# Gate/up tile pairs of a fused MLA decoder layer: six of sixteen k tiles as three 2x2 blocks, with one of four weight sums made by an adding DMA

## The chip, the core and the metric

The kernel runs on one core of a Trainium2 chip. The time is device microseconds of one launch. Engines work beside one another and meet only at semaphores: TensorE (PE) multiplies, ScalarE (ACT) and VectorE (DVE) work on elements, GpSimd (POOL) works on elements and issues software DMAs, SyncE (SP) issues hardware DMAs. A matmul's other half, the load of its 128x128 stationary operand, is PEld.

## What is computed

One layer: sparse latent attention, LayerNorm, SwiGLU, LayerNorm, on 256 tokens of width 2048, all in float32.

```python
def _swiglu(x, w_gate, w_up, w_down):
    return (jax.nn.silu(x @ w_gate) * (x @ w_up)) @ w_down
...
x = _layer_norm(DEEPNORM_ALPHA * x + m, ln1_g, ln1_b)
x = _layer_norm(DEEPNORM_ALPHA * x + _swiglu(x, w_gate, w_up, w_down), ln2_g, ln2_b)
```

The case is about `x @ w_gate` and `x @ w_up`: 256x2048 by 2048x5632, twice.

## The kernel before

**Splitting.** PE multiplies in a reduced float32 form (`float32r`). To keep float32 accuracy each operand is split into a high part and a rest, and each product is three matmuls: high by high, high by low, low by high. For weights, ACT copies the raw float32 block into `w_hi` (the conversion keeps the high part) and DVE then makes `w_lo = raw - w_hi`. So each block of weights goes SP's DMA, ACT, DVE, PE. One split of 128x1024 is a *step*. Steps are numbered by v. `hi_done` and `lo_done` count them. The split weights stand in a ring of four places (`RING`); ACT may fill a place only when PE has finished the step that held it four steps earlier (`used_step(v - RING)`).

**Tiles.** FFN columns go in 22 tiles of 256 gate and 256 up columns (a PSUM bank of 512 for each half of the tokens). Tile 0 and tile 1 are plain: 16 k tiles (128 rows of weights each), as 8 halves of two k tiles. Tiles 2 to 21 go in ten pairs p = 1 to 10 (`first` and `second` tile).

**Pairs.** In a pair, four k tiles (`PAIR_K`) are done as two 2x2 blocks in Winograd's form of Strassen's scheme. Rows of the 2x2 are token halves, columns are the two tiles, the inner index is the two k tiles of a block: seven products (P1, P5, P6, P7, P2, P3, P4) where eight would be needed. Each product is one step and six matmuls, three for each of the two blocks. The other twelve k tiles are plain, two to a step: `first` 0 to 5 and `second` 0 to 5, of 12 matmuls each. That is 7 x 6 + 12 x 12 = 186 matmuls of 128x512 and 19 steps to a pair. The products need four sums of weight blocks, made in place by DVE in `pair_sum` (line 1381), each 128x1024: T1 = B11 + B12, T3 = B12 + B22, T2 = T1 + B22, T4 = B21 + T2 (the minus signs of the scheme lie in the activations' sums and the seeds). P5 takes T1, P6 T2, P7 T3, P4 T4. They also need sums of activations, made once by POOL (lines 1568 to 1580, `g_sum`, `s_gate`).

**Seeds.** P1, P1+P6 and P1+P6+P7 begin other outputs: ACT copies a PSUM bank into another (line 984, semaphore `seeded`), and PE waits for that before it adds there. P5 goes to a bank of its own; ACT takes it out as `y_s` (line 990) and DVE adds it in twice (`add_y`, lines 1398 and 1400).

**Hidden units.** After a tile ends ACT makes the silu (line 935) and DVE multiplies by up (`gate_up`, line 1340). When both tiles of a pair are done DVE transposes them in the next pair in four groups of four 32x256 transposes (`turn_hid`, line 1353; one group after each of the steps `first` 2, 3, 4, 5). The last group raises `ffn_turned`. POOL waits for it and makes four sums for the down projection's own 2x2 blocks (lines 1587 to 1593), later one low part (line 1595), for seven of the pairs; ACT copies the high part (`hid_hi`, line 941), DVE makes the low part (`hid_lo`, line 1359).

**Order.** `ffn_sequence` writes out the order of steps; all engines follow it. The last three steps of a pair's second tile stand between the first products of the next pair. So P1, second 3, P5, second 4, P6, second 5, P7, P2, P3, first 0, P4, first 1 to 5, second 0 to 2, and again. SP's queue is one: plain halves into four places of 512 KB, the blocks of the next pair (two DMAs of 1 MB, `load_quad`) after the plain loads 6 and 7.

Of the kernel before, what the change touches and what calls it, by code (L numbers as in the profile page):

```python
# [24 lines left out]
F32 = mybir.dt.float32  # L25
# [5 lines left out]
P = 128  # L31
# [120 lines left out]
def ffn_sequence():  # L152

    steps = []
    for p in range(1, PAIRS):
        ends = [(p - 1, "second", n) for n in range(PLAIN - 3, PLAIN)] if p > 1 else [None] * 3
# [67 lines left out]
def ring_places():  # L224

    places, at, held, before = [], 2 * (V_DOWN % RING), {}, []
    for u, (_, _, _, width, _) in enumerate(DOWN_UNITS):
        if u >= len(DOWN_UNITS) - LAST_LATE:
            places.append(None)
            before.append(None)  # L230
            continue
        at += at % width
        blocks = [(at + n) % RING_BLOCKS for n in range(width)]
        places.append(blocks[0])
        before.append(max([held[x] for x in blocks if x in held], default=None))
# [34 lines left out]
def layer_kernel(nc, a):  # L270
    ctx = ExitStack()
    with ctx:
# [196 lines left out]
        quad_full = [sem(f"quad_full{i}") for i in range(2)]  # L469
# [3 lines left out]
        pair_t_done = sem("pair_t_done")  # L473
# [28 lines left out]
        down_ring_hi, down_ring_lo = (w[:].rearrange("p r e -> p (r e)") for w in (w_hi, w_lo))  # L502
# [31 lines left out]
        def quad(p, block):  # L534
            return (quad_1 if p == 1 else raw[:, 2:4, :])[:, :, block * GC:(block + 1) * GC]
# [57 lines left out]
        def _(sp):  # L593
# [36 lines left out]
            def load_quad(p, q):  # L630
# [3 lines left out]
                elif p == 2:  # L634
                    sp.wait_ge(lo_done, V_FFN + TILE_HALVES + 4 + 2 * q + 2)
                else:
                    sp.wait_ge(lo_done, V_OF[p - 1, "product", P4] + 1)
                dst = quad_1[:, q, :] if p == 1 else raw[:, 2 + q, :]
                sp.dma_start(dst, w_pairs[p - 1][:, q * RAW_ELEMS:(q + 1) * RAW_ELEMS]).then_inc(quad_full[q], 16)

            def load_plain(p, n):
# [8 lines left out]
                e0 = 2 * RAW_ELEMS + n * HALF  # L650
                sp.dma_start(plain_raw(m), w_pairs[p - 1][:, e0:e0 + HALF]).then_inc(plain_full[m % PLAIN_SLOTS], 16)

            def load_down(b):

                if b < 2:
                    sp.wait_ge(lo_done, V_OF[PAIRS - 1, "product", P4] + 1)
# [10 lines left out]
            load_tile(1)  # L667
            sp.wait_ge(x1_done, TOK * CHUNKS)
# [3 lines left out]
            for p in range(1, PAIRS):  # L672
                for n in range(PLAIN_SLOTS if p == 1 else 0, 2 * PLAIN):
                    load_plain(p, n)
                    if n in (PLAIN, PLAIN + 1):
                        if p < PAIRS - 1:
                            load_quad(p + 1, n - PLAIN)
                        else:
                            load_down(n - PLAIN)
# [25 lines left out]
        def _(act):  # L705
# [225 lines left out]
            def silu_step(i):  # L931
                act.wait_ge(ffn_full, i + 1)
                if i > 1:
# [9 lines left out]
            def tile_1():  # L943
                for h in range(TILE_HALVES):
                    used = used_ffn(0, h + RING) if h < RING else used_ffn(1, h - RING)
                    hi_loop(used, fills(R_FFN + h // 2) + 1, h % 2, h // 2)
                    if h == 3:
                        silu_step(0)
                    if h == 6:
                        act.wait_ge(x1_stored, 16)  # L950
                        act.wait_ge(g_step, 5)
                        act.activation(s_gate[:, 0, :, :, :], g_sum[:], ACT.Copy).then_inc(g_hi, 1)
# [1178 lines left out]
```

## Time and profile before

| | |
|---|---|
| median of 3 runs | 931.21 us (931.13 to 931.63) |
| the profiled execution | 931.67 us, span from first to last instruction 929.9 us |
| PE busy in the span | 923.4 us, 99% |
| DVE busy | 773.7 us, 83% |
| ACT busy | 513.4 us, 55% |
| POOL busy | 95.9 us, 10% |
| DMA | 188.06 MB, mean 202 GB/s |

Busy time is the union of an engine's instructions in the trace. A matmul's row is 389 ns long but matmuls overlap; starts lie closer together than that. The same holds in a smaller way for DVE and ACT: an instruction's row is longer than the distance from its start to the start of the next. Where this document adds up work, it takes the distance of starts and calls it the pitch.

### The profile page before, as it was taken

What the parts mean: (1) busy time and instruction counts of PE and PEld (TensorE: products, weight loads), DVE (VectorE), ACT (ScalarE), POOL (GpSimd) and SP (SyncE); (2) the same over time, 40 slices, a digit from 0 to 9 for tenths busy, and PEclk for the clock granted to TensorE, in tenths of its full rate; (3) what the DMA queues carried; (4) which work ended last, traced back from release to release, by engine and by line L of the source; (5) the groups of instructions that cost most, each with busy time, mean ns of one, the idle gap of its engine ahead of it and who ended that gap; (6) DMA issues with size and microseconds to landing.
All of it is one profiled execution on the core that took longest, in us unless ns stands there. A gap on an engine that the chain in (4) does not pass through costs nothing.

```text
span 929.9 us, 11643 instructions
## 1 busy us (share of the span) xinstructions
PE 923.4 (99%) x4406; PEld 774.5 (83%) x4406; DVE 773.7 (83%) x1049; ACT 513.4 (55%) x704; POOL 95.9 (10%) x84
## 2 busy tenths in 40 slices
PE   9999999999999999999999999999999999999997
PEld 8999988888878888888888888888888888888885
DVE  6778566578779898989999998988969997999777
ACT  5686765354464646555565646455545565456550
POOL 0205530000311020202011020000000000000000
PEclk9999999999999999999999999999999999999999
DMA  9744324584808375665648375756657656355632
GB/s 362 315 166 145 129 91 167 195 328 167 318 5 290 111 256 162 223 218 185 228 135 274 112 270 148 242 198 200 219 210 300 226 225 233 130 222 231 230 132 91
DMA packets 36759, 188.06 MB, mean 202 GB/s; under 512 B 4064, under 2 KB 4576, under 8 KB 22880
## 3 DMA queue, kind: packets, MB, share of 16 engines
q1 hardware_dynamic: 36672, 187.32, 56.4%
q8 instruction: 35, 0.57, 0.3%
q14 instruction: 20, 0.16, 0.1%
q0 software_dynamic: 32, 0.00, 0.0%
HBM read 183.11 MB, written 4.19 MB: 201 GB/s over the span
## 4 chain that ended last, share of the span: by engine, by line
PE 99%; DVE 0%; ACT 0%; DVEq 0%; issue 0%; ACTq 0%
PE acc L1983 26%; PE acc L2005 21%; PE acc L1758 9%; PE tp L1983 9%; PE acc L1966 6%; PE acc L1696 5%; PE tp L1966 4%; PE tp L2005 4%; PE acc L1617 4%; PE acc L1895 2%; PE tp L1935 2%; PE acc L1730 1%; PE tp L1809 1%; PE tp L1744 1%; PE tp L1822 1%; PE tp L1606 0%
## 5 line engine op out<-in xcount | busy, mean ns | idle before, releaser
L1983 PE MATMUL acc<-w_hi,act_t 128*128 128x512 f32 x720 | 227.3, 389 | 0.0
L972 ACT ACTIVATE w_hi<-raw 128x1024 fp32r<-128x1024 f32 x120 | 125.7, 1057 | 111.4 <-PE acc L1983 57.2
L1021 ACT ACTIVATE w_hi<-raw 128x512 fp32r<-128x512 f32 (+1 forms) x154 | 114.9, 782 | 100.3 <-PE acc L2005 88.0
L2005 PE MATMUL acc<-w_hi,hid_t 128*128 128x512 f32 x504 | 161.0, 389 | 0.0
L1424 DVE TENSOR_TENSOR w_lo<-raw,w_hi 128x512 fp32r<-128x512 f32 (+1 forms) x154 | 131.8, 881 | 33.2 <-ACT w_hi L1021 33.0
L1983 PEld LDWEIGHTS acc<-w_hi,act_t 128*128 128x128 f32 x720 | 135.1, 188 | 28.1
L1377 DVE TENSOR_TENSOR w_lo<-raw,w_hi 128x1024 fp32r<-128x1024 f32 x120 | 147.2, 1244 | 7.7 <-ACT w_hi L972 6.9
L1983 PE MATMUL acc<-w_lo,act_t 128*128 128x512 f32 x360 | 140.0, 389 | 0.0
L2005 PEld LDWEIGHTS acc<-w_hi,hid_t 128*128 128x128 f32 x504 | 94.6, 188 | 19.6
L2005 PE MATMUL acc<-w_lo,hid_t 128*128 128x512 f32 x252 | 98.0, 389 | 0.0
L1374 DVE TENSOR_TENSOR w_lo<-raw,w_hi 128x1024 fp32r<-128x1024 f32 x63 | 82.7, 1313 | 18.2 <-ACT w_hi L967 17.8
L967 ACT ACTIVATE w_hi<-raw 128x1024 fp32r<-128x1024 f32 x63 | 66.6, 1057 | 44.8 <-DVE raw L1381 26.4
L1353 DVE STREAM_TRANSPOSE turned<-hid 32x256 f32<-32x256 f32 x176 | 76.8, 436 | 3.9
L1983 PEld LDWEIGHTS acc<-w_lo,act_t 128*128 128x128 f32 x360 | 67.6, 188 | 14.0
L1983 PE MATMUL tp<-w_hi,act_t 128*128 128x512 f32 x240 | 76.7, 389 | 0.0
L1758 PE MATMUL acc<-w_hi,o_t 128*128 128x512 f32 x224 | 73.4, 398 | 0.0
L1206 DVE TENSOR_TENSOR w_lo<-raw,w_hi 128x1024 fp32r<-128x1024 f32 x31 | 41.7, 1360 | 17.5 <-ACT w_hi L874 17.5
L2005 PEld LDWEIGHTS acc<-w_lo,hid_t 128*128 128x128 f32 x252 | 47.3, 188 | 9.9
L1983 PEld LDWEIGHTS tp<-w_hi,act_t 128*128 128x128 f32 x240 | 45.0, 188 | 9.4
L1758 PEld LDWEIGHTS acc<-w_hi,o_t 128*128 128x128 f32 x224 | 42.1, 188 | 8.6
L1983 PE MATMUL tp<-w_lo,act_t 128*128 128x512 f32 x120 | 46.7, 389 | 0.0
L1758 PE MATMUL acc<-w_lo,o_t 128*128 128x512 f32 x112 | 43.6, 390 | 0.0
(262 smaller groups left out, 1582.2 us busy)
## 6 DMA issues: line engine op xcount, KB each, us to landing
raw<-in_w_pairs SPq DMA_DIRECT2D x120, 512.0 KB, 4.5
raw<-in_w_down SPq DMA_DIRECT2D x44, 1024.0 KB, 6.0
raw<-in_w_pairs SPq DMA_DIRECT2D x18, 1024.0 KB, 7.6
raw<-in_w_out SPq DMA_DIRECT2D x16, 1024.0 KB, 4.9
raw<-in_w_gu SPq DMA_DIRECT2D x8, 1024.0 KB, 10.7
raw<-in_x_w SPq DMA_DIRECT2D x14, 552.0 KB, 7.1
raw<-in_w_uq SPq DMA_DIRECT2D x4, 1024.0 KB, 6.1
raw<-in_w_ukv SPq DMA_DIRECT2D x4, 1024.0 KB, 4.8
```

Source lines behind the costliest of these rows:

```text
L967: act.activation(by_quad(w_hi[:, v % RING, :]), quad(p, SOURCE[n]), ACT.Copy).then_inc(hi_done, 1)
L972: act.activation(w_hi[:, v % RING, :], plain_raw(m), ACT.Copy).then_inc(hi_done, 1)
L1021: act.activation(unit_parts(u)[0], block_of(b, block, width), ACT.Copy).then_inc(down_hi_done, 1)
L1353: last = dve.transpose(dst[:, :, :, :, 32 * n:32 * n + 32], src[:, :, :, :, 32 * b:32 * b + 32])
L1374: dve.tensor_tensor(by_quad(w_lo[:, v % RING, :]), quad(p, LOW_OF[n]), by_quad(w_hi[:, v % RING, :]), ALU.subtract).then_inc(lo_done, 1)
L1377: dve.tensor_tensor(w_lo[:, v % RING, :], plain_raw(plain_index(p, kind, n)), w_hi[:, v % RING, :], ALU.subtract).then_inc(lo_done, 1)
L1424: dve.tensor_tensor(lo_, block_of(b, block, width), hi_, ALU.subtract).then_inc(down_lo_done, 1)
L1696: last = pe.matmul(out, part[:, v % RING, e0:e0 + P], act_tiles[:, k, x, :], start=(half == 0 and k == 0 and x == 0 and part is hi_), stop ...
L1758: last = pe.matmul(acc[:, bank0 + t, :], lhs[:, k, x, t * P:(t + 1) * P], part[:, w, n * GC:(n + 1) * GC], start=(start and x == 0 and par ...
L1966: last = pe.matmul(out, factor(q, Q_FACTOR[n], x), part[:, v % RING, q * GC:(q + 1) * GC], start=(start and (q, x) == (0, 0) and part is w ...
L1983: last = pe.matmul(out[:, t, :], act_t[:, k0 + m, x, t * P:(t + 1) * P], part[:, v % RING, m * GC:(m + 1) * GC], start=False, stop=(end an ...
L2005: last = pe.matmul(bank, lhs(x), part[:, cols * GC:(cols + 1) * GC], start=(first == u and (cols, x) == (0, 0) and part is hi_), stop=(end ...
```

## The change

`PAIR_K` becomes 6: three 2x2 blocks and ten plain k tiles. A product is now two steps, `two` (blocks 0 and 1, 128x1024, six matmuls) and `third` (block 2, 128x512, three matmuls). Plain steps are `first` 0 to 4 and `second` 0 to 4. The ring is cut into eight places of 512 columns, handed out by `ring_places`; `BEFORE[v]` is the last step that held any of v's places, and `FREED[v]` the first step that needs one of v's. ACT's seeds and silus and DVE's `gate_up` hang on `FREED`.

The order changes: P1, second 1, P2, second 2, P5, second 3, P6, second 4, P7, P3, first 0, P4, first 1 to 4, second 0. The transposes stand after first 2, 3, 4 and second 0 (`TURN_STEPS`), so the last group is directly ahead of the next pair's P1 on DVE. The first pair's products stand between halves 4 to 7 of tile 1.

T1 is made by a DMA with `accum_op=ALU.add` that POOL issues from the weights in HBM onto the block in SBUF, 512 KB for blocks 0 and 1 and 256 KB for block 2. ACT's P5 waits for it. T3, T2 and T4 are made by DVE after the steps of P2, P5 and P6. POOL's loop over pairs is now `load_t1`, then the low part of the sums of two pairs ago, then `factor_sums`. The activations' sums have three blocks. SP loads three blocks of 1 MB for a pair, from just after first 0.

```diff
-        for product, end in zip((P1, P5, P6), ends):
-            steps += [(p, "product", product), end]
-        steps += [(p, "product", n) for n in (P7, P2, P3)] + [(p, "first", 0), (p, "product", P4)]
-        steps += [(p, "first", n) for n in range(1, PLAIN)] + [(p, "second", n) for n in range(PLAIN - 3)]
+        for product, end in zip((P1, P2, P5, P6), range(1, PLAIN)):
+            steps += [(p, "two", product), (p, "third", product), (p - 1, "second", end)]
+        steps += [(p, part, product) for product in (P7, P3) for part in ("two", "third")]
+        steps += [(p, "first", 0), (p, "two", P4), (p, "third", P4)]
+        steps += [(p, "first", n) for n in range(1, PLAIN)] + [(p, "second", 0)]
...
+TURN_STEPS = ("first", 2), ("first", 3), ("first", 4), ("second", 0)
...
-                    if n in (PLAIN, PLAIN + 1):
-                        if p < PAIRS - 1:
-                            load_quad(p + 1, n - PLAIN)
+                    if n == PLAIN_SLOTS and p < PAIRS - 1:
+                        load_quad(p + 1, 0)
+                        load_quad(p + 1, 1)
+                    if n == PLAIN_SLOTS + 1 and p < PAIRS - 1:
+                        load_quad(p + 1, 2)
...
+                elif n == P5:
+                    act.wait_ge(t1_two if kind == "two" else t1_third, 16 * p)
...
-                if (kind, n) == ("product", P1):
-                    pair_sum(p, B11, B11, B12)
-                    pair_sum(p, B12, B12, B22)
-                if (kind, n) == ("product", P5):
-                    pair_sum(p, B11, B11, B22)
-                if (kind, n) == ("product", P2):
-                    pair_sum(p, B21, B11, B21)
-                if (kind, n) == ("first", 2):
+                if n == P2 and kind in ("two", "third"):
+                    sum_3(p, kind)
+                if n == P5 and kind in ("two", "third"):
+                    sum_2(p, kind)
+                if n == P6 and kind in ("two", "third"):
+                    sum_4(p, kind)
+                if (kind, n) == ("first", 1):
                     add_y(p)
...
+            def load_t1(p):
+
+                blocks = w_pairs[p - 1][:, 0:BLOCKS * RAW_ELEMS].rearrange("p (q e) -> p q e", q=BLOCKS)
+                b12 = blocks[:, :, B12 * GC:(B12 + 1) * GC]
+                pool.wait_ge(lo_done, V_OF[p, "two", P1] + 1)
+                pool.dma_start(two(p, B11), b12[:, 0:2, :], accum_op=ALU.add).then_inc(t1_two, 16)
+                pool.wait_ge(lo_done, V_OF[p, "third", P1] + 1)
+                pool.dma_start(third(p, B11), b12[:, 2, :], accum_op=ALU.add).then_inc(t1_third, 16)
...
+            for p in range(1, PAIRS):
+                load_t1(p)
+                if p == 1:
+                    pool.wait_ge(g_hi, 1)
...
+                if 0 <= p - 2 < len(DOWN_QUADS):
+                    factor_low(p - 2)
+                if p - 1 < len(DOWN_QUADS):
+                    factor_sums(p - 1)
```

## Rows read from the trace of the kernel before

**Rows 1.** The page: busy per engine, then the chain that ended last.

```profile
PE 923.4 (99%) x4406; PEld 774.5 (83%) x4406; DVE 773.7 (83%) x1049; ACT 513.4 (55%) x704; POOL 95.9 (10%) x84
...
PE 99%; DVE 0%; ACT 0%; DVEq 0%; issue 0%; ACTq 0%
```

**Rows 2.** Busy time by stretch of 42 us, one pair each; the columns are named.

```profile
core 0: us, PE busy (x) PEld busy (x) DVE busy (x) ACT busy (x) POOL busy (x), PEclk, DMA share, GB/s
440.00:482.00 42.00, 42.00 (x187) 34.79 (x186) 38.88 (x44) 23.82 (x28) 6.11 (x5) 1.00 0.60 199
566.00:608.00 42.00, 42.00 (x187) 34.79 (x186) 37.78 (x44) 23.44 (x27) 0.00 (x0) 1.00 0.61 202
```

**Rows 3.** Timeline of ACT: start, length, engine, line, operation [idle before, releaser].

```profile
412.08 1.06 ACT L972 ACTIVATE w_hi<-raw 128x1024 fp32r<-128x1024 f32 x1 [1.66 <-PE acc L1983]
414.80 1.06 ACT L972 ACTIVATE w_hi<-raw 128x1024 fp32r<-128x1024 f32 x1 [1.66 <-PE acc L1983]
418.50 1.06 ACT L972 ACTIVATE w_hi<-raw 128x1024 fp32r<-128x1024 f32 x1 [2.64 <-DMA raw<-in_w_pairs]
...
429.20 1.06 ACT L967 ACTIVATE w_hi<-raw 128x1024 fp32r<-128x1024 f32 x1 [2.27 <-DVE raw L1381]
...
444.75 0.59 ACT L984 ACTIVATE acc<-acc 128x512 f32<-128x512 f32 x1
```

**Rows 4.** Timeline of POOL: two pairs' sums, and the low part between.

```profile
420.56 1.44 POOL L1587 TENSOR_TENSOR s_sum<-turned 128x128 f32<-128x128 f32 x1 [30.29 <-DVE turned L1353]
422.08 1.32 POOL L1589 TENSOR_TENSOR turned<-turned 128x128 f32<-128x128 f32 x1
423.48 1.36 POOL L1591 TENSOR_TENSOR s_sum<-turned 128x128 f32<-128x128 f32 x1
424.92 0.47 POOL L1593 TENSOR_TENSOR s_sum<-turned,s_sum 128x128 f32<-128x128 f32 x1
430.75 1.56 POOL L1595 TENSOR_TENSOR s_t<-s_sum,s_t 128x384 fp32r<-128x384 f32 x1 [5.36 <-ACT s_t L1005]
462.72 1.43 POOL L1587 TENSOR_TENSOR s_sum<-turned 128x128 f32<-128x128 f32 x1 [30.40 <-DVE turned L1353]
```

**Rows 5.** Timeline of DVE over the products of a pair.

```profile
425.68 1.22 DVE L1359 TENSOR_TENSOR hid_t<-turned,hid_t 128x1024 fp32r<-128x1024 f32 x1
426.81 1.22 DVE L1374 TENSOR_TENSOR w_lo<-raw,w_hi 128x1024 fp32r<-128x1024 f32 x1
427.95 2.35 DVE L1381 TENSOR_TENSOR raw<-raw 128x1024 f32<-128x1024 f32 x2
430.22 1.22 DVE L1377 TENSOR_TENSOR w_lo<-raw,w_hi 128x1024 fp32r<-128x1024 f32 x1
431.35 2.04 DVE L1374 TENSOR_TENSOR w_lo<-raw,w_hi 128x1024 fp32r<-128x1024 f32 x1
```

**Rows 6.** Timeline of DVE: the transposes of one pair, and what follows.

```profile
411.25 1.23 DVE L1377 TENSOR_TENSOR w_lo<-raw,w_hi 128x1024 fp32r<-128x1024 f32 x1
412.51 1.79 DVE L1353 STREAM_TRANSPOSE turned<-hid 32x256 f32<-32x256 f32 x4
414.31 1.22 DVE L1377 TENSOR_TENSOR w_lo<-raw,w_hi 128x1024 fp32r<-128x1024 f32 x1
...
420.45 2.63 DVE L1377 TENSOR_TENSOR w_lo<-raw,w_hi 128x1024 fp32r<-128x1024 f32 x2
```

**Rows 7.** Timeline of DVE in the first pair: `add_y`.

```profile
281.48 0.69 DVE L1398 TENSOR_TENSOR acc<-y_s,acc 128x512 f32<-128x512 f32 x1
282.07 0.69 DVE L1400 TENSOR_TENSOR acc<-y_s,acc 128x512 f32<-128x512 f32 x1
282.87 1.77 DVE L1353 STREAM_TRANSPOSE turned<-hid 32x256 f32<-32x256 f32 x4
```

**Rows 8.** DMA issues: what, queue, count, KB each, median us from issue to landing.

```profile
raw<-in_w_pairs SPq DMA_DIRECT2D x120, 512.0 KB, 4.5
raw<-in_w_pairs SPq DMA_DIRECT2D x18, 1024.0 KB, 7.6
...
out<-x SPq DMA_DIRECT2D x2, 128.0 KB, 2.1
rms_g<-in_rms_g_t POOLq DMA_DIRECT2D x1, 3.0 KB, 3.8
```

**Rows 9.** Tile `raw`, stretch 375 to 465 us: DMAs from issue to landing.

```profile
DMA to landing us min/median/max: 3.5/4.8/8.1
```

**Rows 10.** Timeline of POOL: the activations' sums, ahead of the first pair.

```profile
243.75 2.41 POOL L1568 TENSOR_TENSOR x_t<-act_t 128x1024 f32<-128x1024 f32 x1 [112.38 <-DVE act_t L1288]
246.23 1.60 POOL L1573 TENSOR_TENSOR g_sum<-x_t 128x256 f32<-128x256 f32 x1
...
251.28 1.60 POOL L1578 TENSOR_TENSOR g_sum<-x_t,g_sum 128x256 f32<-128x256 f32 x1
```

**Rows 11.** Line 1966, PE's products: length in ns, first and last start.

```profile
L1966 PE MATMUL acc<-w_hi,act_t x100: 389/389/395, 269.4 to 661.8; 128*128 128x512 f32 x100
```

More of the change, by code:

```diff
@@ L655, in load_down @@
                 if b < 2:
-                    sp.wait_ge(lo_done, V_OF[PAIRS - 1, "product", P4] + 1)
+                    sp.wait_ge(lo_done, V_OF[PAIRS - 1, "two", P4] + 1)
                 elif b < RING:
@@ L999, in _ @@
                 hi_step(p, kind, n)
-                if (kind, n) == ("second", PLAIN - 4):
+                if (p, kind, n) == (0, "second", 1):
+                    gate_sums_hi()
+                if (kind, n) == ("second", 2) and p > 0:
                     hid_hi(p - 1)
-                if (kind, n) == ("product", P5) and 2 <= p < len(DOWN_QUADS) + 2:
+                if (kind, n) == ("third", P5) and 2 <= p < len(DOWN_QUADS) + 2:
                     q = p - 2
@@ new lines, in lo_step, with sum_2, sum_3 @@
+                    dve.tensor_tensor(ring_lo[:, cols], src, ring_hi[:, cols], ALU.subtract).then_inc(lo_done, 1)
+            def sum_2(p, kind):
+                part = two if kind == "two" else third
+                dve.tensor_tensor(part(p, B11), part(p, B11), part(p, B22), ALU.add).then_inc(t2_done, 1)
+            def sum_3(p, kind):
+                part = two if kind == "two" else third
+                dve.tensor_tensor(part(p, B12), part(p, B12), part(p, B22), ALU.add).then_inc(t3_done, 1)
@@ L1383, in before_lo, with sum_4 @@
+            def sum_4(p, kind):
+                part = two if kind == "two" else third
+                dve.wait_ge(t2_done, 2 * (p - 1) + (1 if kind == "two" else 2))
+                dve.tensor_tensor(part(p, B21), part(p, B11), part(p, B21), ALU.add).then_inc(t4_done, 1)
             def before_lo(v):
-                if v - RING in FFN_ENDS:
-                    gate_up(2 + FFN_ENDS.index(v - RING))
-                if v - RING == V_PAIRS - 1:
-                    gate_up(1)
+                for i, end in enumerate(FFN_ENDS):
+                    if v == FREED[end]:
+                        gate_up(1 + i)
@@ L1400, in add_y @@
                 dve.tensor_tensor(second[:, 1, :], y_s[:], second[:, 1, :], ALU.subtract).then_inc(y_added, 1)
-            tile_1()
+            for h in range(HALVES_1):
+                lo_loop(V_FFN + TILE_HALVES + h, h % 2, h // 2)
+                if h == 3:
+                    gate_up(0)
             for p, kind, n in FFN_STEPS:
@@ L1988, in _ @@
             first_tile()
-            tile_1()
+            for h in range(HALVES_1):
+                pe.wait_ge(lo_done, V_FFN + TILE_HALVES + h + 1)
+                half_1(h, slice(h % RING * HALF, (h % RING + 1) * HALF))
             for p, kind, n in FFN_STEPS:
-                if kind == "product":
-                    pair_product(p, n)
+                if kind in ("two", "third"):
+                    pair_product(p, kind, n)
+                elif p == 0:
+                    pe.wait_ge(lo_done, V_OF[p, kind, n] + 1)
+                    half_1(HALVES_1 + n - 1, ring(V_OF[p, kind, n], 2))
                 else:
```

287 lines of the change are left out of this document (159 added, 128 removed).

## The prediction

> **What bounds the kernel now.** I read the page first. PE is busy 99% of the span and the chain that ended last is PE for 99% [rows 1]. Nothing stands between matmuls, so the time falls only with the number of matmuls, and rises as soon as anything makes PE wait. DVE is next with 83%, but that is a mean over stages. In the stretches of the pairs (270 to 692 us) DVE is busy 38.9 of 42 us where POOL works too and 37.8 where it doesn't [rows 2]. So DVE has some 3 us of rest in a pair; the 1.1 us between the two is what DVE loses to POOL. One place shows it: the low step at 431.35 takes 2.04 us instead of 1.22, beside POOL's operation at 430.75 [rows 4, 5]. ACT has much rest. It mostly waits for PE to free a place of the ring [rows 3]: that is a full ring, and PE is fed. The reader should see that PE sets the pace and DVE follows it closely.
>
> **Pitches.** A pair takes 42.16 us from POOL row to POOL row, 420.56 to 462.72 [rows 4]. With 186 matmuls that is 0.2267 us each, and 2.72 us for a plain step of twelve, as two ACT rows show, 412.08 and 414.80 [rows 3]. DVE at 1024 columns has a pitch of 1.14 us, for low steps and for sums alike (427.95 to 430.22 for two sums) [rows 5]. At 512 columns it is 0.60 (281.48 to 282.07) and `add_y` as a whole is 1.39 [rows 7]. A plain step with a transpose group behind it is 3.06 us (411.25 to 414.31) [rows 6].
>
> **PE's part.** A third block saves 3 matmuls of 24: per pair 63 + 120 = 183 for 186. Ten pairs, 30 matmuls, 30 x 0.2267 = 6.8 us off PE. A pair is then 41.5 us. Smaller steps cost PE nothing that a row shows: its matmuls run on across steps.
>
> **DVE's part.** Low steps: before 19 x 1.14; after 17 x 1.14 and 7 x 0.60. Sums: before 4 x 1.14; after 3 x 1.14 and 3 x 0.60. That is from 26.2 to 28.8 us a pair. The rest (four plain-with-transpose surcharges of 1.92 = 7.7, `hid_lo` 1.14, two `gate_up` 1.2, `add_y` 1.4) stays, 11.4 us. The method gives 37.6 for before without POOL, and the row says 37.8 [rows 2]. After it gives 40.2, and 41.3 with POOL's 1.1. PE needs 41.5. DVE just fits, but whatever makes it idle now lengthens the pair. That is the point on which all hangs.
>
> **ACT's part.** Per pair 17 copies of 1024 (pitch about 1.0) and 7 of about 0.55 for 19 copies: 2 us more on an engine busy 24 of 42 us [rows 2]. The third seed is close: ACT makes it after silu, two copies and `y_s`, all behind PE's end of second 4, and PE wants it 2.7 us after P7's first part. Added by rows of 0.6 and 1.0 it comes at about 2.3. I take 0 for it; 0 to 3 us in all is its bound.
>
> **T1's part.** DVE is rid of T1, but T1 is now the end of a chain. In the order of DVE the last transpose group comes directly ahead of P1. It raises `ffn_turned`, and POOL, which has waited, begins its four sums. They take from 420.45 to 425.39, 4.9 us, because DVE's operations are in the way [rows 4, 6]. Only then does POOL come to `load_t1`. The low part of P1 has long been made by then. The DMA takes D; ACT's P5 waits for it, copies in 1.06 us and then DVE makes the low part: 1.1 us with the semaphores [rows 3]. Behind the waiting copy ACT has the rest of the product steps, and DVE, working in order, has only third P1, second 1, P2 with T3, second 2 and `hid_lo`: 0.60 + 1.14 + 3.48 + 1.14 + 1.14 = 7.5 us after P1, near 10 after `ffn_turned` with what POOL takes. The DMA's chain is 4.9 + D + 1.1, so above D = 4 DVE idles.
>
> From P5's low part to the next `ffn_turned` DVE has P5 and T2 3.48, second 3 1.14, P6 and T4 3.48, second 4 1.14, P7 1.74, P3 1.74, `gate_up` and first 0 1.74, P4 1.74, first 1 and `add_y` 2.53, and four times 3.06: 31.0. With the 0.8 that POOL's low part costs it is 31.8. **The cycle is 31.8 + 4.9 + D + 1.1 = 37.8 + D.** It beats PE's 41.5 from D = 3.7 on.
>
> **D.** The trace has no adding DMA. Nearest rows: 512 KB from SP, median 4.5 us [rows 8], fastest 3.5, slowest 8.1 [rows 9]; 128 KB from SP 2.1; 3 KB from POOL 3.8 [rows 8]. Going by these, POOL's queue starts at 3.8, and the step from 128 to 512 KB adds 1.4: 5.2. An add must also read what is there; if that costs as much again, 6.6. Bounds: 3.5, as fast as SP's fastest, and 9.8, SP's slowest with POOL's surplus of 1.7. I take 6.2. The second DMA (256 KB) lands later, but third P5 is wanted 2.3 us later; I take it at nothing.
>
> A rule speaks for a smaller D. The Trainium skill's page DMA: Bandwidth & Descriptors, section Anatomy of one DMA, gives a GpSimd-issued DMA as 2.0 us plus bytes over 436e3, an estimate of 3.2 us here; the cycle would be 41.0 and PE would stay the bound. The one POOL row, 3.8 us for 3 KB, stands against it. The page Collectives: The Full Stack, section The bandwidth ceiling, says that a reducing transfer is slower because it needs two reads; no row here shows one.
>
> **The sum.** With D = 6.2 the cycle is 44.0, 2.5 over PE. It holds from pair to pair where POOL's sums stand ahead of T1, pairs 2 to 8: six cycles from P5 of pair 2 to P5 of pair 8, 15.0 us. Off goes the lead at the start. The products began at 269.4 [rows 11] and now begin four plain steps earlier, 258.5; P5 is 42 matmuls on, 268.0, and in pair 2 309.5. POOL's activation sums ended at 252.9 [rows 10] and are half as wide again, so T1 goes out at about 256; P5's low part starts at 263.3, the next at 263.3 + 31.0 + 4.9 + 6.2 + 1.1 = 306.5, and is done 1.3 later at 307.8. Lead 1.7. Behind a late P5 PE also meets T2 on DVE's queue ahead of third P5, some 1.5 us once. Pairs 9 and 10 have no sums: cycle 31.8 + 1.1 + 6.2 + 1.1 = 40.2, no loss. The profiled execution was 931.67: 931.67 - 6.8 + 15.0 - 1.7 + 1.5 = 939.7. The median lies 0.46 below it: 939.2 us.
>
> **Other edits.** The activations' sums cost DVE about 1 us of contention more ahead of pair 1; DVE waits for PE there, so nothing, at most 1. Block loads are 3 MB within 15 us. They begin earlier, at P4, and land before P1 if 1 MB takes 7.6 us in a row of them [rows 8]; ACT's present waits for plain loads, 2.6 us [rows 3], are covered by the ring. The down stage is untouched.
>
> **Rivals.**
> *T1 is hidden.* D is 4 or less, or little more. For it: SP's 512 KB row has 3.5 as its least and the page's figure is lower still. Against: the POOL row. Then PE stays the bound and all 6.8 us come: 931.2 - 6.8 = 924.4. This is the other side, and it decides from D = 5 down: there six cycles of 1.3 us over PE, with 1.5 behind and at most 2.4 of lead off (a full ring gives no more), are as much as the 6.8 gained.
> *DVE is the bound by its load alone.* T1 comes early enough, but 41.3 of 41.5 us leaves no room for waits between dense product steps. At 0.3 to 0.6 us a pair: 927 to 931.
> *The adding transfer is slow.* D of 8 or more, for the second read or for the plain loads beside it. D = 8.5: cycle 46.3, six times 4.8 = 29, pairs 9 and 10 one us each, 1.5 behind, no lead: 931.2 - 6.8 + 32.5 = 957.
> *It doesn't do what it says.* If the DMA were not adding beside the engines but POOL held DVE while it writes descriptors, DVE would lose about 1 us a pair: 934. Part of the forecast's range.
>
> **Chances.** Forecast (D from 5 to 7.5, 931 to 950) 0.50; T1 hidden 0.22; DVE's load 0.12; slow transfer 0.16. About 0.2% is what a measurement of this kernel can tell from no change, 929.3 to 933.1. Faster: 0.22 and half of 0.12, 0.28. Same: the other half and the low end of the forecast, 0.08. Slower: 0.64. Range: from the hidden case, 924, to D = 8.5, 957.
>
> **What would show it.** Right: ACT's P5 copy waits for the adding DMA in pairs 2 to 8, some 2 us or more each; DVE idles before P5; POOL issues T1 behind its four sums; PE idles at P5 in pairs 3 to 8 and not in 9 and 10; POOL-to-POOL distance 44 us. T1 hidden: that distance is 41.5 and PE shows no idle. DVE's load: PE waits on DVE's low parts at many steps, DVE's share over 97%, and no wait for the DMA. Wrong altogether: PE waits at a seed, or ACT at a block load.

## The result

The changed kernel takes 966.3 us (four runs, 964.6 to 969.1) against 931.2 before: a ratio of 1.038 (95% interval 1.035 to 1.040), 35 us slower. I had forecast 939.2 and a range up to 957. The sign was right, the size was not: the loss is more than four times the 8 us that I gave, and outside the range.

The page of the changed kernel, the parts that answer to [rows 1] and [rows 8]:

```profile
PE 936.1 (97%) x4376; PEld 771.4 (80%) x4376; DVE 804.2 (83%) x1119; ACT 530.8 (55%) x755; POOL 120.0 (12%) x105
...
PE 68%; DVE 18%; DMA 6%; POOL 3%; ACT 2%; issue 2%; DVEq 0%; ACTq 0%; POOLq 0%
...
raw<-in_w_pairs SPq DMA_DIRECT2D x100, 512.0 KB, 4.7
...
raw<-in_w_pairs POOLq DMA_DIRECT2D x9, 512.0 KB, 7.4
```

PE has 30 matmuls less (4376) and yet more busy time: some ran slower. The chain that ended last was PE for 99%; now over a quarter of it (27%) is DVE, DMA and POOL. T1's DMA took 7.4 us (median of nine; 7.3 with the first pair's), where I had put 6.2. DVE's share of the span is the same 83%, so the engine that I had called near its limit looks unchanged; it is the order of waits that tells.

Busy time of each engine by stretch, one pair each, to be read beside [rows 2]:

```profile
core 0: us, PE busy (x) PEld busy (x) DVE busy (x) ACT busy (x) POOL busy (x), PEclk, DMA share, GB/s
...
393.00:439.50 46.50, 42.49 (x185) 33.96 (x184) 41.60 (x52) 25.43 (x32) 8.01 (x7) 1.00 0.61 199
...
534.00:582.00 48.00, 45.31 (x185) 35.65 (x184) 41.70 (x52) 25.43 (x32) 7.69 (x7) 0.93 0.59 193
```

A pair is 46.5 us in one and 48.0 in the other, against 42.16. DVE is busy 41.6 of them: my 41.3 held. It is idle 5 us in the first and 6 in the second. Pairs 9 and 10, without POOL's sums, take 43.1 and 42.1. The down stage starts at 727.2 instead of 692.0: all 35 us are lost ahead of it, nearly all in the pairs.

The chain itself, in the stretch 393 to 412 us, from the timelines of POOL, ACT, DVE and PE (start, length, engine, line, operation, idle before and its releaser):

```profile
393.42 1.43 POOL L1652 TENSOR_TENSOR s_sum<-turned 128x128 f32<-128x128 f32 x1 [30.35 <-DVE turned L1394]
...
397.61 1.21 POOL L1643 DMA_DIRECT2D raw<-in_w_pairs  x1
...
405.25 1.06 ACT L998 ACTIVATE w_hi<-raw 128x1024 fp32r<-128x1024 f32 x1 [5.62 <-DMA raw<-in_w_pairs]
...
406.33 1.22 DVE L1410 TENSOR_TENSOR w_lo<-raw,w_hi 128x1024 fp32r<-128x1024 f32 x1 [2.98 <-ACT w_hi L998]
...
407.70 0.47 PE L2049 MATMUL tp<-w_hi,s_gate 128*128 128x512 f32 x1 [2.40 <-DVE w_lo L1410]
...
410.17 0.50 PE L2049 MATMUL tp<-w_hi,s_third 128*128 128x512 f32 x1 [0.84 <-DVE w_lo L1414]
...
411.91 0.50 PE L2067 MATMUL acc<-w_hi,act_t 128*128 128x512 f32 x1 [0.78 <-DVE w_lo L1420]
```

Read from the top: POOL starts its sums with the last transpose, issues T1 4.2 us later, the DMA lands after 7.6, ACT has waited 5.6 us for it, DVE 3.0, PE 2.4 and twice 0.8 more on the dense steps behind. That is the forecast's chain, link by link; the sizes come below.

### The profile page after: what moved, and what is told of

The parts are those of the page before. It is cut to its first block, busy times and chain, and to the rows that moved or that the text cites. A ratio compares the mean times of both kernels' runs of the same rounds, so it can differ in the third digit from the quotient of the medians.

```text
span 965.0 us, 11746 instructions
## 1 busy us (share of the span) xinstructions
PE 936.1 (97%) x4376; PEld 771.4 (80%) x4376; DVE 804.2 (83%) x1119; ACT 530.8 (55%) x755; POOL 120.0 (12%) x105
## 4 chain that ended last, share of the span: by engine, by line
PE 68%; DVE 18%; DMA 6%; POOL 3%; ACT 2%; issue 2%; DVEq 0%; ACTq 0%; POOLq 0%
PE acc L2094 20%; PE acc L1838 9%; PE acc L2067 7%; DMA raw<-in_w_pairs 6%; DVE turned L1394 6%; DVE w_lo L1420 5%; PE acc L1776 5%; PE tp L2067 4%; PE tp L2094 4%; PE acc L1697 4%; PE tp L2049 3%; PE acc L2049 3%; PE tp L2013 2%; DVE w_lo L1410 2%; PE acc L1975 2%
## 5 line engine op out<-in xcount | busy, mean ns | idle before, releaser
L2067 PE MATMUL acc<-w_hi,act_t 128*128 128x512 f32 x600 | 194.4, 394 | 2.4 <-DVE w_lo L1420 2.2
L1480 DVE TENSOR_TENSOR w_lo<-raw,w_hi 128x512 fp32r<-128x512 f32 (+1 forms) x154 | 131.9, 882 | 31.9 <-ACT w_hi L1062 31.8
L1013 ACT ACTIVATE w_hi<-raw 128x1024 fp32r<-128x1024 f32 x100 | 105.0, 1055 | 71.8 <-PE acc L2067 35.4
L2067 PEld LDWEIGHTS acc<-w_hi,act_t 128*128 128x128 f32 x600 | 113.5, 189 | 32.3 <-DVE w_lo L1420 6.8
L1420 DVE TENSOR_TENSOR w_lo<-raw,w_hi 128x1024 fp32r<-128x1024 f32 x104 | 128.4, 1236 | 11.5 <-ACT w_hi L1013 9.2
L2067 PE MATMUL acc<-w_lo,act_t 128*128 128x512 f32 x300 | 117.6, 392 | 0.0
L998 ACT ACTIVATE w_hi<-raw 128x1024 fp32r<-128x1024 f32 x63 | 66.5, 1056 | 73.7 <-DMA raw<-in_w_pairs 39.5
L1410 DVE TENSOR_TENSOR w_lo<-raw,w_hi 128x1024 fp32r<-128x1024 f32 x63 | 78.9, 1252 | 25.3 <-ACT w_hi L998 25.1
L1394 DVE STREAM_TRANSPOSE turned<-hid 32x256 f32<-32x256 f32 x176 | 76.7, 436 | 2.9
L2067 PE MATMUL tp<-w_hi,act_t 128*128 128x512 f32 x200 | 67.1, 400 | 0.7 <-DVE w_lo L1420 0.4
L2067 PEld LDWEIGHTS acc<-w_lo,act_t 128*128 128x128 f32 x300 | 56.8, 189 | 11.2
L2049 PE MATMUL tp<-w_hi,s_gate 128*128 128x512 f32 x100 | 38.1, 423 | 15.3 <-DVE w_lo L1410 15.3
L2049 PE MATMUL acc<-w_hi,act_t 128*128 128x512 f32 x150 | 50.5, 390 | 0.2 <-DVE w_lo L1414 0.2
L1414 DVE TENSOR_TENSOR w_lo<-third_raw,w_hi 128x512 fp32r<-128x512 f32 x63 | 50.7, 805 | 0.0
L1247 DVE TENSOR_TENSOR w_lo<-raw,w_hi 128x1024 fp32r<-128x1024 f32 x27 | 38.1, 1428 | 14.2 <-ACT w_hi L893 14.2
L1001 ACT ACTIVATE w_hi<-third_raw 128x512 fp32r<-128x512 f32 x63 | 39.4, 625 | 18.6 <-DMA third_raw<-in_w_pairs 9.9
```

The lines of the kernel that those rows point to most:

```text
L998: act.activation(by_quad(ring_hi[:, ring(v, 2)]), two(p, SOURCE[n]), ACT.Copy)\
L1013: act.activation(ring_hi[:, ring(v, 2)], plain_raw(m), ACT.Copy).then_inc(hi_done, 1)
L1394: last = dve.transpose(dst[:, :, :, :, 32 * n:32 * n + 32], src[:, :, :, :, 32 * b:32 * b + 32])
L1410: dve.tensor_tensor(by_quad(ring_lo[:, cols]), two(p, LOW_OF[n]), by_quad(ring_hi[:, cols]), ALU.subtract).then_inc(lo_done, 1)
L1414: dve.tensor_tensor(ring_lo[:, cols], third(p, LOW_OF[n]), ring_hi[:, cols], ALU.subtract).then_inc(lo_done, 1)
L1420: dve.tensor_tensor(ring_lo[:, cols], src, ring_hi[:, cols], ALU.subtract).then_inc(lo_done, 1)
```

## The experiments

Each is timed beside the kernel before, which took 931.0 to 931.8 us each time. "The pair" is the distance from one pair's last transposes on DVE to the next pair's, unless said otherwise.

**T1's DMA ahead of POOL's sums.**

```diff
                 if 0 <= p - 2 < len(DOWN_QUADS):
+                    factor_sums(p - 2)
                     factor_low(p - 2)
-                if p - 1 < len(DOWN_QUADS):
-                    factor_sums(p - 1)
```

> Only POOL's order changes: it issues T1's two adding DMAs of a pair first and makes the four activation sums of the pair before after them. Theory of the wait (the loss is the chain from the last transpose over POOL's sums and the DMA to P5): T1 goes out 3.1 us earlier (1.2 instead of 4.3 us after the last transpose), the pair goes from 46.5 to about 43.4 us in pairs 2 to 8, PE's stalls at P5 nearly vanish and with them the stretches at the lower granted clock; 935 to 944 us. Theory of DVE's load (17 + 7 low steps and six sums are too dense, wherever T1 comes from): nothing changes, 960 us or more.

Measured 947.6 us, ratio 1.017 (1.016 to 1.019). So 18.7 us came from T1 standing behind the sums, and with them the lower clock went (1.000 instead of 0.988). ACT waits 6.3 us in all for T1 instead of 39.5. But the time is above the 944 that I gave: a pair is 44.1 us, not 43.4. ACT still waits 13.8 us in all for T1's second DMA (256 KB), yet DVE does not idle for it: from the last transposes (387.50) up to `gate_up` (413.99) it has no gap. Six of its rows there are long, 2.2 us in all, beside POOL's sums and low part. So T1's DMA no longer sets the pair here; DVE's own work and its waits do.

**T1 left out.**

```diff
-                elif n == P5:
-                    act.wait_ge(t1_two if kind == "two" else t1_third, 16 * p)
...
-                load_t1(p)
```

> T1's DMAs and ACT's wait for them are left out, so P5, P6 and P4 take a block without the sum (that part of the computation is left out). Theory of the wait: PE is the bound again, a pair is 41.5 us, PE idles nowhere, 924 to 927 us. Theory of DVE's load: DVE is busy 41 us or more of each pair and its small waits lengthen the pair to 43 us or more; 940 us or more.

Measured 941.9 us, 1.011 (1.010 to 1.013). These are the numbers of the theory of DVE's load (a pair of 43 us or more, 940 or more); the theory of the wait alone, 924 to 927, is out. Even so T1's chain costs 24.4 us of the 41.9 over what PE's work would give (924.4), and 17.5 stay without it. A pair is 43.4 us. Timeline of DVE in that kernel, behind the last transposes:

```profile
386.84 1.23 DVE L1408 TENSOR_TENSOR w_lo<-raw,w_hi 128x1024 fp32r<-128x1024 f32 x1
387.98 0.95 DVE L1412 TENSOR_TENSOR w_lo<-third_raw,w_hi 128x512 fp32r<-128x512 f32 x1
388.86 0.68 DVE L1379 TENSOR_TENSOR hid<-hid,acc 128x512 f32<-128x512 f32 x1
389.45 1.43 DVE L1418 TENSOR_TENSOR w_lo<-raw,w_hi 128x1024 fp32r<-128x1024 f32 x1
390.81 1.48 DVE L1408 TENSOR_TENSOR w_lo<-raw,w_hi 128x1024 fp32r<-128x1024 f32 x1
...
396.82 2.03 DVE L1408 TENSOR_TENSOR w_lo<-raw,w_hi 128x1024 fp32r<-128x1024 f32 x1
...
410.83 0.69 DVE L1379 TENSOR_TENSOR hid<-hid,acc 128x512 f32<-128x512 f32 x1 [0.42 <-ACT hid L956]
411.78 1.23 DVE L1418 TENSOR_TENSOR w_lo<-raw,w_hi 128x1024 fp32r<-128x1024 f32 x1 [0.26 <-ACT w_hi L1011]
413.21 1.23 DVE L1408 TENSOR_TENSOR w_lo<-raw,w_hi 128x1024 fp32r<-128x1024 f32 x1 [0.20 <-ACT w_hi L996]
```

DVE runs 23.6 us without a gap, from P1 to P3. Four of its rows are long, 0.95, 1.43, 1.48 and 2.03 for 0.68, 1.22, 1.22 and 1.22: POOL's sums and low part lie beside them, 1.5 us a pair. Then come five gaps of 0.15 to 0.54 us, 1.6 in all (three of them in the rows above). The first hangs on PE: ACT has waited 1.14 us for the end of second 4 before its silu, `gate_up` waits for that, and first 0 is behind it.

**The add as such.** Both DMAs of T1 alike:

```diff
-                pool.dma_start(two(p, B11), b12[:, 0:2, :], accum_op=ALU.add).then_inc(t1_two, 16)
+                pool.dma_start(two(p, B11), b12[:, 0:2, :]).then_inc(t1_two, 16)
```

> The two DMAs that POOL issues copy B12 over B11 instead of adding it (so the sum T1 is left out); size, queue, waits and order are the same. If the add costs a second read: landing falls from 7.4 us to about 5.5, which is 1.9 us in each of eight pairs, 945 to 953 us. If the 7.4 us are those of the software queue and the size: landing stays at 7 us or more and the time within 3 us of 966.

Measured 948.3 us, 1.018 (1.016 to 1.019), 18.0 below the changed kernel and as the theory of the second read had it. The DMAs' own rows in the changed kernel and in this one:

```profile
L1643 POOL DMA_DIRECT2D raw<-in_w_pairs x9: 1205/1225/1236, 304.8 to 673.6; - x9
...
DMA to landing us min/median/max: 6.1/7.3/7.6
```

```profile
L1643 POOL DMA_DIRECT2D raw<-in_w_pairs x9: 721/729/738, 304.0 to 655.8; - x9
...
DMA to landing us min/median/max: 4.1/5.1/5.4
```

The add costs 2.2 us in landing, of which 0.5 is the issue on POOL (1.23 for 0.73). In the seven pairs where POOL's sums stand ahead that is 15.4 of the 18.0 us: here each microsecond of the DMA is one of the pair. The mean granted clock rises as well, from 0.988 to 0.998.

**T1 by DVE**, no DMA:

```diff
+                if n == P1 and kind in ("two", "third"):
+                    sum_1(p, kind)
...
-                load_t1(p)
```

> Three blocks and the new order stay, but T1 too is made by DVE, right after the low steps of P1 (1.14 + 0.60 us more), and POOL issues no DMA. Theory of the wait: nothing waits for a DMA any more; DVE's work is 40.2 + 1.7 + 1.1 us, so DVE becomes the bound at about 43 us a pair with its few waits; 938 to 946 us. Theory of DVE's load: worse than with the DMA, above 966 us, since DVE has yet more to do.

Measured 952.6 us, 1.022 (1.021 to 1.024). Better than the DMA by 13.7, so the load theory's ranking is wrong, but 6.6 above the top of my range for the other. Three blocks with all sums on DVE lose 21 us to the kernel with two.

**One part alone: T1 by the DMA in the kernel with two blocks.**

```diff
+                pool.wait_ge(lo_done, V_OF[p, "product", P1] + 1)
+                pool.dma_start(quad(p, B11), blocks[:, :, B12 * GC:(B12 + 1) * GC], accum_op=ALU.add)\
+                    .then_inc(t1_two, 16)
...
-                    pair_sum(p, B11, B11, B12)
```

> One part alone: the kernel before with its two blocks and its order, but T1 made by POOL's adding DMA (512 KB) after the low part of P1. P5 follows P1 after one plain step here, so ACT waits for the DMA. Theory of the wait: DVE has only T3 and one plain low step (2.3 us) while the DMA takes 7 us and the copy 1; DVE idles some 6 us a pair, of which its rest of 4 us and the sum's 1.1 us cover most; PE loses 1 to 3 us a pair, 942 to 960 us. Theory that the load alone does it: DVE has 1.1 us less to do than before, 931 us.

Measured 970.0 us, 1.040 (1.039 to 1.042). The DMA alone loses 39 us, more than the whole change; I had 960 at most. DVE waits 76.7 us in all for copies of product steps (17.8 in the kernel before); the DMA (6.1 us) has only one plain step and T3 beside it. POOL's sums are done before T1 is issued here, so they add nothing to the chain, but DVE has less to do while the DMA runs. (The edit also puts POOL's low part of a pair behind the next pair's T1.) From this I take it that the new order, with P2 and a plain step more between P1 and P5, was worth having for T1; no run has the new order with two blocks, so that is argued and not shown.

**POOL's sums small, with T1's DMA and without it.**

```diff
-                pool.tensor_tensor(s_sum[:, S3, :], a11, a21, ALU.subtract).then_inc(s_step, 1)
+                pool.tensor_tensor(s_sum[:, S3, 0:n], a11[:, 0:n], a21[:, 0:n], ALU.subtract).then_inc(s_step, 1)
```

> The changed kernel with POOL's four activation sums of pairs 2 to 7 made on one column of 128 (that part of the sums is left out); T1's adding DMA stays behind them. Theory of the chain (last transpose, POOL's sums, DMA, copy, low steps): the sums shrink from 4.3 to about 2.6 us and the pair from 46.5 to about 44.8 us in six pairs; with the stretches at the lower clock gone 950 to 956 us. If what counts is only the port that the sums hold, 0.9 us a pair: 960 us. If the transfer's length alone counts: 966 us.

Measured 956.8 us, 1.027 (1.026 to 1.029). T1 goes out 2.4 to 2.5 us after the first sum's start instead of 4.2, and the six pairs are 44.8 to 46.7 us, 45.6 on average. I had 44.8 and at most 956: the chain's side, 0.8 us too high. The DMA itself was slower here, 7.7 us in the median for 7.4, and in some pairs the clock fell (mean 0.996).

> As t1_left_out (T1's sum is left out), and POOL's four activation sums of pairs 2 to 7 are made on one column of 128 instead of all (that part is left out too), so they hardly hold the port that DVE's low steps need. The pair was 43.4 us there, of which DVE's rows show some 0.9 us lost beside the four sums. If DVE's total work is the bound: pairs 2 to 7 fall to 42.5 us, 935 to 938 us. If the bound is the exchange between DVE and PE behind the product steps: no more than 1 us in all, 941 us.

Measured 932.3 us, 1.0012 (1.0002 to 1.0021). More than I expected (935 to 938): 9.6 us less than t1_left_out, the pair 41.9 us for 43.4. In its DVE timeline the four long rows are gone:

```profile
386.76 0.69 DVE L1412 TENSOR_TENSOR w_lo<-third_raw,w_hi 128x512 fp32r<-128x512 f32 x1
387.36 0.68 DVE L1379 TENSOR_TENSOR hid<-hid,acc 128x512 f32<-128x512 f32 x1
387.96 1.22 DVE L1418 TENSOR_TENSOR w_lo<-raw,w_hi 128x1024 fp32r<-128x1024 f32 x1
389.09 1.22 DVE L1408 TENSOR_TENSOR w_lo<-raw,w_hi 128x1024 fp32r<-128x1024 f32 x1
...
394.84 1.22 DVE L1408 TENSOR_TENSOR w_lo<-raw,w_hi 128x1024 fp32r<-128x1024 f32 x1
```

DVE was the bound there, and 1.6 us less of it is 1.6 us less of the pair. The Trainium skill's page SBUF — State Buffer, section Who interferes with whom, says that a VectorE instruction with two SBUF inputs contends with a GpSimd instruction that reads SBUF; the rows of 1.48 and 2.03 beside 1.22 agree. Even so this kernel, free of T1 and of most of POOL's sums, does not reach 924: eight of its pairs are 41.9 to 42.5 us, not 41.5.

Three kernels in which DVE never waits for T1 can now be set side by side. From the last transposes of one pair to those of the next, DVE's only gaps are the same five, 1.6 us in all, and the rest is its work, laid end to end:

| | DVE's work | its gaps | the pair |
|---|---|---|---|
| t1_out_small_sums | 40.3 | 1.6 | 41.9 |
| t1_left_out | 41.8 | 1.6 | 43.4 |
| t1_before_sums | 42.5 | 1.6 | 44.1 |

The work differs by the rows that POOL lengthens. In the first row it is the 40.2 us that I had put for DVE without POOL. So DVE's work and its waits together are above PE's 41.5 in all three.

**The chain shifted by one low step.**

```diff
-TURN_STEPS = ("first", 2), ("first", 3), ("first", 4), ("second", 0)
+TURN_STEPS = ("first", 1), ("first", 2), ("first", 3), ("first", 4)
```

> The changed kernel with the four transpose groups one step earlier and nothing else. Theory of the chain (last transpose, POOL's sums, T1's DMA, copy, DVE's steps up to the next last transpose): one low step of 1.1 to 1.2 us leaves the chain, six to eight times, 956 to 960 us. If the order of the transposes is of no matter to the chain: 966 us.

Measured 959.4 us, 1.030 (1.028 to 1.032), as the chain says. The transposes stand a low step of 1.14 us earlier; in six or seven pairs that is 6.8 to 8.0 us, and 6.9 were gained. (The DMA took 7.7 us in the median here, for 7.4.)

**T1 out first, and the last transposes behind P1.**

```diff
-                if (kind, n) in TURN_STEPS and p > 0:
+                if (kind, n) in TURN_STEPS[:3] and p > 0:
...
+                if (kind, n) == ("third", P1) and p > 1 or (p, kind, n) == (PAIRS - 1, "second", 0):
+                    turn_hid(p - 1 if kind == "second" else p - 2, 3)
```

> As t1_before_sums (947.6), and DVE's last transpose group is moved behind the low steps of P1, so T1 goes out 1.8 us earlier relative to DVE's work. If T1's DMA is still in the chain there: 8 pairs less 1 us or more each until the load's 43.4 us is met, 940 to 943 us. If only the load bounds t1_before_sums: unchanged, 947 us.

Measured 948.0 us, 1.018 (1.016 to 1.019), like t1_before_sums. ACT no longer waits for T1's DMA of 512 KB at all, and nothing is gained. That agrees with the load as the bound there. But the silu of the next tile now waits for the later transposes (32 us in all, 16 before), so this is no clean test.

**Other sums by DMA.** DVE makes T1 and T2; adding DMAs make T3 (from HBM) and T4 (from SBUF), both far ahead of their use (the added lines that issue them):

```diff
+                pool.dma_start(two(p, B12), b22[:, 0:2, :], accum_op=ALU.add).then_inc(t3_two, 16)
...
+                pool.dma_start(two(p, B21), two(p, B11), accum_op=ALU.add).then_inc(t4_two, 16)
```

> Three blocks, the new order, but the sums are dealt out otherwise: DVE makes T1 and T2, adding DMAs make T3 (B22 from HBM onto B12, issued after T1, wanted at P7 some 15 us later) and T4 (T2 from SBUF onto B21, issued after T2, wanted at P4 some 10 us later). DVE has 1.7 us less to do than in t1_left_out, 40.1 us a pair, and no chain waits for a transfer. If both theories hold (a transfer in a chain costs, DVE's load costs) PE is the bound: 925 to 932 us. If the software DMAs themselves slow DVE or PE: 938 us or more.

Measured 946.4 us, 1.016 (1.014 to 1.018): a miss. I had 925 to 932, or 938 and more if the DMAs slowed an engine; it is slower, but not for that reason. No engine waits for these DMAs, but T1 now stands on DVE between P1 and second 1. PE's timeline there, and the busy times of the engines in the two stretches of 5 us beside it, then in the 5 us behind the same wait one pair earlier (columns as above):

```profile
394.33 0.53 PE L2070 MATMUL acc<-w_hi,act_t 128*128 128x512 f32 x1 [1.62 <-DVE w_lo L1422]
```

```profile
390.00:395.00 5.00, 3.38 (x14) 2.32 (x13) 5.00 (x6) 3.96 (x5) 4.83 (x5) 0.97 0.07 9
395.00:400.00 5.00, 5.00 (x17) 3.89 (x16) 3.29 (x4) 0.96 (x1) 0.00 (x0) 0.69 1.00 226
...
350.77:355.77 5.00, 5.00 (x22) 4.15 (x23) 4.74 (x5) 2.05 (x4) 0.66 (x1) 1.00 0.94 193
```

PE waits once in each of nine pairs, 1.6 us in seven and 1.0 in the last two. Behind the wait shown it has 17 matmuls in 5 us where a dense stretch has 24, at a granted clock of 0.69. But that is not the rule: the clock fell behind three of the seven waits of 1.6 us (at 305, 394 and 527) and stayed at 1.00 behind the other four, one of which is the last line. Where the two kinds can be compared, the pair is 45.2 us with the fall and 43.6 to 43.9 without: the wait costs nearly as much again in clock, when the clock falls.

T1 moved behind second 1 (against the kernel just described):

```diff
-                if n == P1 and kind in ("two", "third"):
-                    sum_1(p, kind)
...
+                if (kind, n) == ("second", 1) and p < PAIRS - 1:
+                    sum_1(p + 1, "two")
+                    sum_1(p + 1, "third")
```

> As t3_t4_dma (946.4), with DVE's T1 moved from behind the low steps of P1 to behind that of second 1. There PE waited 1.6 us at second 1, once in each of nine pairs, and ran at the lower granted clock after it. If that wait is the whole of what is left over 925: it goes, 925 to 931 us. If the software DMAs or DVE's load hold the pair at 43 us or more: 940 us or more.

Measured 937.9 us, 1.008 (1.006 to 1.009). The wait at second 1 and the low clock are gone, 8.5 us, but not all: a pair is 42.6 us or a little more, with DVE busy from `gate_up` (409.73) to behind second 1's low step (433.14) but for 1.2 us, and PE waiting 0.35 us or less at a time within the pairs.

Then T4 back on DVE, so that one sum is by DMA as in the change, but T3 in T1's place:

> One sum of four by a DMA, as in the change, but another one: T3, which nothing waits for within 15 us. DVE makes T1 (behind second 1), T2 and T4. DVE's work is as in t1_left_out plus nothing, 41.8 us and 1.6 us of small waits a pair: 936 to 943 us by the theory of DVE's load, 925 to 931 us if the loss of t1_left_out came from the place of the sums and not from their number.

Measured 942.7 us, 1.013 (1.012 to 1.015), as DVE's load says: the pair is 43.4 us as in t1_left_out. It is 23.6 us faster than the change, with as many sums by a DMA. Which sum the DMA makes matters more than that it makes one.

Last, T3 and T4 by DMA again and T1 on DVE behind P2, without and with `TURN_STEPS` a step earlier:

```diff
+                if (kind, n) == ("third", P2):
+                    sum_1(p, "two")
+                    sum_1(p, "third")
```

> As t3_t4_dma_t1_later (937.9), with DVE's T1 moved once more, from ahead of the low steps of P2 to behind them. There the pair is 42.6 us, and PE waits some 0.8 us a pair at P2. If that is the exchange between PE and DVE that is left: 42.0 us or less a pair, 929 to 934 us. If not, unchanged at 938 us.

> As t1_behind_p2, and all four transpose groups one step earlier (behind first 1 to 4), so the silu of the first tile, which waits for the last group, and second 1 behind it come earlier. ACT waits 16 us in all for the transposes there. If second 1 is late for that reason: 1 to 4 us less than t1_behind_p2. If DVE's work up to second 1 sets it, in whatever order: the same within 1 us.

Measured 938.6 and 938.4 us, 1.008 and 1.007 (1.006 to 1.010): both the same as t3_t4_dma_t1_later: the 929 to 934 that I had as one side did not come. Shifting T1 and the transposes about on DVE gives nothing more. None of these kernels beats the one before.

## Why the prediction was wrong

**PE's part, right.** 30 matmuls fewer, and 0.2267 us each where PE is fed at full clock.

**The mechanism, right.** The cycle from the last transposes over POOL's sums, the DMA and P5 back to the last transposes bounds pairs 2 to 8. Four experiments moved one link each (small_sums, t1_plain_copy, turn_early, t1_before_sums) and the time followed. What failed is the length of the cycle, the number of cycles and the clock. I had 14.8 us over PE's work, 15.0 less 1.7 and plus 1.5; it was 41.9.

**The cycle, mis-sized: 46.5 us for 44.0.** Link by link in the stretch above: POOL's sums 4.3 for 4.9 (two of the four rows are long, 1.43 and 1.32, where three were before); D 7.6 for 6.2; copy 1.1; DVE from P5's low part (406.33) to the last transposes' end (439.8) 33.4 for 31.8. The last is the term I judged worst. I had added DVE's pitches and left out its waits in that stretch. They are the idle times in these rows, 1.6 us in all:

```profile
420.37 0.69 DVE L1381 TENSOR_TENSOR hid<-hid,acc 128x512 f32<-128x512 f32 x1 [0.43 <-ACT hid L956]
421.32 1.23 DVE L1420 TENSOR_TENSOR w_lo<-raw,w_hi 128x1024 fp32r<-128x1024 f32 x1 [0.26 <-ACT w_hi L1013]
422.76 1.22 DVE L1410 TENSOR_TENSOR w_lo<-raw,w_hi 128x1024 fp32r<-128x1024 f32 x1 [0.21 <-ACT w_hi L998]
...
424.74 1.22 DVE L1420 TENSOR_TENSOR w_lo<-raw,w_hi 128x1024 fp32r<-128x1024 f32 x1 [0.15 <-ACT w_hi L1013]
...
427.69 1.23 DVE L1420 TENSOR_TENSOR w_lo<-raw,w_hi 128x1024 fp32r<-128x1024 f32 x1 [0.53 <-ACT w_hi L1013]
```

The first comes from PE: silu waits for the end of second 4, and `gate_up` for silu. The next three are copies that ACT makes behind that silu. The last is a copy that waited 1.90 us for PE to free a place. A late P5 is not needed for them: the same five gaps, 1.6 to 1.7 us, stand in pair 1 (281 to 288 us), ahead of any late P5, and in t1_left_out and t1_out_small_sums. They belong to the order of the steps. I had set such waits at nothing for the forecast and at 0.3 to 0.6 for the rival.

**D.** My middle leaned on 5.2 without the add and 6.6 with it. Without, it was 5.1; the add put on 2.2 and not 1.4. The estimate of 3.2 us, by the formula of the Trainium skill's page DMA: Bandwidth & Descriptors, section Anatomy of one DMA, is too low here: even the plain copy took 4.1 to 5.4 us, and the measurement decides.

**The lead, wrong.** I took 1.7 us off. The first cycle, 298.69 to 345.22 us by the last transposes, is already 46.5. DVE started P5 of pair 1 at 267.7, not 263.3. ACT's copy had to wait until 264.6 for PE to free a place, and DVE still had P2 and T3 ahead, whose two long rows took 2.35 and 2.30 us for 1.22 beside POOL's operations on `s_gate` and `s_third` (259.76 to 264.40). I had put that contention at nothing. So seven cycles count, not six, at 5.0 over PE each: 35 us where I had 15.0 less 1.7.

**The clock, not thought of.** I priced a stall at its own length. Stretches of the changed kernel in the pair of 48.0 us:

```profile
546.00:550.00 4.00, 1.74 (x7) 1.19 (x6) 2.87 (x3) 3.38 (x5) 1.20 (x1) 0.93 0.34 126
550.00:554.00 4.00, 3.58 (x8) 1.94 (x7) 4.00 (x5) 2.30 (x3) 0.36 (x1) 0.50 0.16 18
554.00:558.00 4.00, 4.00 (x14) 3.11 (x14) 3.26 (x4) 0.53 (x1) 0.00 (x0) 0.72 0.30 113
```

From 546 to 550 PE does only 7 matmuls, since it waits for P5. In the next 4 us it does 8 at a granted clock of 0.50, the lower of its two levels (1.2 of 2.4 GHz), and then 14 at 0.72, where 19 are done at full clock. The two pairs in which this stands are 48.0 and 47.7 us, the other five 46.3 to 46.7: 2.7 us more in all. In three of the five the clock falls too, for less long (0.61 in 362 to 366, 1.00 behind it), and the pair is no longer than those at 1.00 throughout. t3_t4_dma shows the fall behind three of seven waits of 1.6 us. In t1_before_sums, t1_left_out and t3_t4_dma_t1_later the mean clock is 1.000 and no such stretch is seen.

**Pairs 9 and 10, nearly right.** 43.1 and 42.1 us where I had 41.5: 2.2 us.

**The account.** PE's work alone gives 924.4, the kernel takes 41.9 more. Seven cycles at 5.0 over PE are 35, the clock 2.7, pairs 9 and 10 2.2: 39.9, and 2.0 are left. Some 1.5 of them stand ahead of the first late P5: PE's starts lie 0.9 us too far apart at 248.60 and 1.5 at 266.13 and 267.87, where the kernel before has only 0.9, at 274.29. By what the experiments take away: T1's chain with its clock 24.4 (t1_left_out), POOL's sums 9.6 (t1_out_small_sums), and 7.9 stay with neither. The two accounts do not divide the loss in the same way: without T1 the pair is still bound at 43.4, by DVE's work and its waits.

**DVE's load, under-priced.** I gave this rival 0.3 to 0.6 us a pair and 927 to 931. It is real: with T1 gone, the pair is 43.4 us and the time 941.9, worse than my forecast of the whole. DVE had 41.3 of 41.5 us, and I took its waits for small. But what it waits for is PE, by way of silu and `gate_up`, and PE waits for it; of two engines at the limit each gives its waits to the other. With 40.2 us of work by my own sum and 1.6 of waits it was over PE's 41.5 even before POOL. POOL's price was 1.5 us of lengthened rows where I had 1.1. My sign for this rival, a share of DVE over 97%, could not have shown it: the waits keep the share below that.

**The range.** Its high end, 957, came from the slow transfer alone (D = 8.5). D was 7.4 in the median and 7.6 at most, inside the range; the cycle was long because the other term was. The rival's high end had no bound for DVE's waits, though the rows of the gaps could have been set against the load.

**What held.** No wait of note at a seed; DVE and PE never late for a block load (ACT waited 4.9 us in nine pairs for the third block, and nothing behind it did); POOL issued T1 behind its sums; PE waited at P5 in seven pairs. That POOL's DMA would hold DVE while it is written does not show: in pair 9, where T1 goes out without sums (630.54 us), the DVE rows beside it have their usual 0.68 and 1.22 us.

**The last 7.9 us.** They are what t1_out_small_sums keeps over PE's work, and its trace places 7.5 of them: 1.5 at the start as above, 2.2 in the cycle behind pair 1's sums, which are made in full there (43.7 us), and 3.8 in eight pairs of 41.9 to 42.5 us, DVE's work and waits once more.

**What stays open.** Why T1's DMA is slower in the changed kernel (median 7.4 us) than ahead of the sums (6.0) is not known. Nor is what decides whether the clock falls behind a wait of 1.6 to 2.4 us. What the new order does to the kernel with two blocks was not run. t1_early_turn_late is no clean test of its link.

## What to carry to other kernels

When a change brings a second engine to within a per cent of the bound one, add up its waits on the bound engine too, not its work alone: here that was 1.6 us a pair that the sum left out. Such waits can be read before the change is made, as idle times in the rows of the second engine. A DMA that stands in a cycle from one round of the loop to the next costs its whole issue-to-landing time in each round for as long as that cycle is the bound. Give it to an operand that is wanted long after it can go out (T3 in place of T1 gave back 23.6 us), or put it ahead of other work in its queue (T1 ahead of POOL's sums gave back 18.7).

## What was new about the hardware

- An adding DMA of 512 KB from POOL takes 6.0 us (median in t1_before_sums) to 7.4 (changed kernel) or 7.7 (small_sums), 5.1 as a plain copy; its issue occupies POOL for 1.23 us, the plain one for 0.73.
- In this kernel a POOL operation on SBUF beside a DVE operation with two inputs in SBUF went with a longer DVE row: 0.95 for 0.68 us, 1.43 to 2.03 for 1.22.
- A short wait of PE between dense steps was followed by a lower granted clock in some pairs and not in others. Behind waits of 1.6 us it was 0.66 over the next 5 us three times and 1.00 four times (t3_t4_dma). Behind waits of 1.8 to 2.4 us it fell in five pairs of seven (changed kernel), to 0.50 and then 0.72 over two times 4 us in the longest pair. In t3_t4_dma the fall cost some 1.5 us a pair; in three pairs of the changed kernel, where it was soon back at 1.00, it cost nothing that shows in the pair's time.
